# Two transformer blocks on one core: where the modulation's sums, the first attention steps and thirty adds of squares stand

## What is computed

```python
for l in range(2):                                     # first_block
    mod_x = silu(c) @ w_ada[l] + b_ada[l]              # 6 * 1024 columns
    mod_c = silu(c_ctx) @ w_ada[l] + b_ada[l]
    q, k, v... = modulate(rms_norm(x, g_norm1[l]), sh1, sc1) @ w_in[l]
    x = x + gt1 * (attention heads of three kinds @ w_out[l])
    x = x + gt2 * conv_ffn(modulate(rms_norm(x, g_norm2[l]), sh2, sc2), w_up, conv_w, w_down)
for l in range(2):                                     # second_block, 272 tokens
    h = h + 0.5 * rmsnorm(swiglu(rmsnorm(h, g_pre_ffn1[l]), ...), g_post_ffn1[l])
    h = h + rmsnorm(token_mixer(rmsnorm(h, g_pre_mix[l]), ...), g_post_mix[l])
    h = h + 0.5 * rmsnorm(swiglu(rmsnorm(h, g_pre_ffn2[l]), ...), g_post_ffn2[l])
```

## Time and profile before

| | |
|---|---|
| time, median of 3 runs | 2470.73 us (2468.18 to 2471.03) |
| the profiled execution | 2474.26 us, its span 2472.5 |
| mean granted TensorE clock | 0.975 |
| PE busy | 2346.7 us (95%) |
| DVE, ACT, POOL busy | 62%, 53%, 17% |
| wl splits (L1796) | 574, mean 1349 ns |
| POOL products (L744) | 50 of products_a, mean 2809 ns; 46 of products_b, mean 2642 ns |

### The profile page before, as it was taken

How to read it: one execution, slowest core, us unless ns; L and a number is a source line. 1 busy time by engine, 2 the same in 40 slices (tenths; PEclk the granted TensorE clock), 3 DMA queues, 4 the chain that set the end, 5 groups by cost and what they waited for, 6 DMA issues and landing times.

```text
span 2472.5 us, 46933 instructions
## 1 busy us (share of the span) xinstructions
PE 2346.7 (95%) x17349; PEld 2129.3 (86%) x17349; DVE 1530.2 (62%) x2405; ACT 1316.3 (53%) x2439; POOL 408.2 (17%) x348
## 2 busy tenths in 40 slices
PE   7999989999887999999999999999999999998998
PEld 5786768888665878999999888999999998898998
DVE  5436586666555555885665774676556647666764
ACT  4536556665555464655444646454454445555553
POOL 1214465652882031000000000000000000000000
PEclk9999989999998999999999999999999998999999
DMA  7750133434443302556555432445545563344654
GB/s 298 225 171 10 35 127 133 145 139 121 143 152 116 95 26 81 176 173 183 168 173 170 146 107 99 154 162 178 174 134 188 168 183 107 103 156 143 194 178 130
DMA packets 101200, 356.43 MB, mean 144 GB/s; under 512 B 11344, under 2 KB 13040, under 8 KB 101072
## 3 DMA queue, kind: packets, MB, share of 16 engines
q1 hardware_dynamic: 86704, 304.45, 38.2%
q0 software_dynamic: 14368, 50.24, 6.2%
HBM read 352.55 MB, written 1.05 MB: 143 GB/s over the span
## 4 chain that ended last, share of the span: by engine, by line
PE 76%; DVE 9%; POOL 5%; issue 4%; ACT 4%; DMA 1%; DVEq 1%; ACTq 0%; SPq 0%; POOLq 0%
PE ps L783 19%; PE ps L785 19%; PE ps L784 19%; POOL products_b L744 4%; DVE wl L1796 3%; PE ps L800 2%; PE ps L801 2%; PE ps L804 2%; PE ps L923 2%; PE ps L938 2%; PE ps L909 2%; ACT wh L1321 1%; DMA ada_raw<-in_w_ada 1%; PE ps L845 1%; DVE conv L2387 1%
## 5 line engine op out<-in xcount | busy, mean ns | idle before, releaser
L1796 DVE TENSOR_TENSOR wl<-raw,wh 128x1024 fp32r<-128x1024 f32 x574 | 773.5, 1349 | 560.7 <-ACT wh L1321 559.6
L783 PE MATMUL ps<-hH,wh 128*128 128x272 f32 (+2 forms) x2864 | 886.3, 309 | 9.5 <-DVE silu L2435 3.1
L784 PE MATMUL ps<-hL,wh 128*128 128x272 f32 (+2 forms) x2864 | 872.1, 305 | 0.0
L785 PE MATMUL ps<-hH,wl 128*128 128x272 f32 (+2 forms) x2864 | 871.9, 304 | 0.0
L1321 ACT ACTIVATE wh<-raw 128x1024 fp32r<-128x1024 f32 x574 | 602.3, 1052 | 256.9 <-PE ps L785 231.8
L783 PEld LDWEIGHTS ps<-hH,wh 128*128 128x128 f32 x2864 | 543.2, 190 | 41.6 <-issue 8.3
L784 PEld LDWEIGHTS ps<-hL,wh 128*128 128x128 f32 x2864 | 543.3, 190 | 19.9 <-issue 0.5
L785 PEld LDWEIGHTS ps<-hH,wl 128*128 128x128 f32 x2864 | 543.4, 190 | 19.0
L783 PE MATMUL ps<-actH,wh 128*128 128x272 f32 (+2 forms) x1136 | 347.9, 306 | 20.0 <-DVE wl L1796 19.0
L785 PE MATMUL ps<-actH,wl 128*128 128x272 f32 (+2 forms) x1136 | 347.3, 306 | 0.0
L784 PE MATMUL ps<-actL,wh 128*128 128x272 f32 (+2 forms) x1136 | 346.2, 305 | 0.0
(11 more groups left out here) (308 smaller groups left out, 3224.0 us busy)
## 6 DMA issues: line engine op xcount, KB each, us to landing
raw<-in_w_ffn_gu SPq DMA_DIRECT2D x176, 512.0 KB, 3.5
raw<-in_w_mix SPq DMA_DIRECT2D x98, 512.0 KB, 3.5
raw<-in_w_up SPq DMA_DIRECT2D x88, 512.0 KB, 3.5
raw<-in_w_ffn_down SPq DMA_DIRECT2D x64, 512.0 KB, 3.5
ada_rest<-in_w_ada POOLq DMA_DIRECT2D x32, 512.0 KB, 4.6
raw<-in_w_out SPq DMA_DIRECT2D x32, 512.0 KB, 3.4
raw<-in_w_down SPq DMA_DIRECT2D x32, 512.0 KB, 3.5
raw<-in_w_qk SPq DMA_DIRECT2D x26, 512.0 KB, 4.3
```

The lines of the kernel that those rows point to most:

```text
L783: pe.matmul(out, a_h, b_h, start=start, stop=False)
L784: pe.matmul(out, a_h, b_l, start=False, stop=False)
L785: return pe.matmul(out, a_l, b_h, start=False, stop=stop)
L1796: dve.tensor_tensor(wl[:, slot, :], raw[:, slot, :], wh[:, slot, :].bitcast(F32), ALU.subtract).then_inc(l_split, 1)
```

## The change

Three things. The modulation's sums are placed anew: three in out0 (steps 2, 4, 6), 28 in up0 (four in the first turn, three in each of the eight turns behind it) and 17 in down0 (two in three steps, and step 2); `SUM_EARLY` goes from 25 to 31. In attention, layer 0 has two early steps as layer 1 has, the second one's scores go to banks 2 and 3, and the attention's start waits for four tiles of v instead of five. And the six adds of squares of the five later pre-norms move from DVE to POOL (`add_squares`), each waiting for the add before it and for its square; POOL's memsets of the mixer's tables stand behind them.

```diff
--- before.py
+++ after.py
@@ -48,8 +48,9 @@
 ADA_FIRST = 2 * KT
 EARLY = 3
 RAW_AT = 8
-SUM_OUT, SUM_UP = 7, 18
-SUM_EARLY = SUM_OUT + SUM_UP
+SUM_OUT, SUM_UP = 3, 18
+SUM_EARLY = SUM_OUT + 3 * SUM_UP // 2 + 1
+SUM_DOWN = [j for j in range(24) if j % 3 < 2 or j == 2]
 DOWN_PARTS = (8, 8, 6)
 TILES2 = ((0, 16), (16, 128), (144, 128))
 GLA_LEVELS = 7
...
+        square_pooled = sem("square_pooled")
@@ -526,8 +528,8 @@
                 p = PAIRS[idx]
                 self.p, self.idx, self.qt, self.diff, self.m = p, idx, qt, p >= 6, m
                 self.n, self.g, self.bank = n, PAIR_STEPS[0] * l + n, 6 + idx % 2
-                self.early = n <= l
-                self.scores = 4 + 2 * n if self.early else 2 * (n % 2)
+                self.early = n <= 1
+                self.scores = 4 if n == 0 else 6 if l and n == 1 else 2 * (n % 2)
                 self.nk, self.k0 = (T1, 0) if qt < 2 else (TC, TX)
                 self.opens, self.closes = m == 0, p < 6 or m == 1
                 self.first, self.last = qt == 0 and m == 0, ends
@@ -756,6 +758,22 @@
                             pool.dma_start(weights[:, i % 2, :] if i < SUM_EARLY else weights_b[:, i % 2, :],
                                            io["w_ada"][1, i]).then_inc(weights_loaded[i % 2], 16)
 
+            squares_before = [0]
+
+            def add_squares(n):
+
+                for k in range(1, KT - 1):
+                    pool.wait_ge(sq_ready, 8 * n.idx + k + 1)
+                    if k > 1:
+                        pool.wait_ge(square_pooled, squares_before[0])
+                    ins = pool.tensor_tensor(n.nrstd[:, 0, n.lo:], n.nsq[:, 0, n.lo:] if k == 1 else n.nrstd[:, 0, n.lo:],
+                                             n.nsq[:, k, n.lo:], ALU.add)
+                    if k == KT - 2:
+                        ins.then_inc(sum_ready, 1)
+                    else:
+                        squares_before[0] += 1
+                        ins.then_inc(square_pooled, 1)
+
             pool.wait_ge(h_ready, 24)
             pool.dma_start(xT[:, :, X2:X0], io["metaT"].rearrange("(k p) t -> p k t", p=P)).then_inc(meta_loaded, 16)
             for l in range(2):
@@ -764,7 +782,7 @@
                 for dst, name in ((mask[:, T2 - P:T2], "causal"), (lmask[:], "lmask"), (wal[32:48], "wal%d" % l)):
                     src = io["w_alpha"][l].rearrange("r (t c) -> r t c", c=P) if name.startswith("wal") else io[name]
                     pool.dma_start(dst, src).then_inc(mix_tables, 16)
-                pool.wait_ge(x_tile, 8 * post_before[norms["post_ffn1", l].idx] + 8)
+                add_squares(norms["pre_mix", l])
                 pool.memset(xlev[:, 0], 1.0).then_inc(pool_set, 1)
                 pool.memset(xlev[:, 1], 1.0).then_inc(pool_set, 1)
                 pool.memset(cum_hl[:].bitcast(F32), 0.0).then_inc(pool_set, 1)
@@ -772,6 +790,9 @@
                 pool.memset(att[:], 0.0).then_inc(pool_set, 1)
                 pool.memset(att0[0:NMETA], 0.0).then_inc(pool_set, 1)
                 pool.memset(mask[:, 0:T2 - P], 0.0).then_inc(pool_set, 1)
+                add_squares(norms["pre_ffn2", l])
+                if l == 0:
+                    add_squares(norms["pre_ffn1", 1])
 
 
 
@@ -901,8 +922,10 @@
             def pair_attention(l):
                 def scores(st):
 
-                    if st.n >= 4 or st.n + l == 3:
+                    if st.n >= 4 - (l == 0):
                         pe.wait_ge(pair_exp, st.g - 1)
+                    if st.n == 2 + l:
+                        pe.wait_ge(*after_tile(S[f"v{l}"], 4))
                     b = st.scores
                     for qi, ki in ((0, 0), (0, 1), (1, 0)):
                         for c in range(2):
@@ -949,6 +972,8 @@
                         pe.wait_ge(qk_low, N_HEADT * l + 6)
                         pe.wait_ge(roped, N_ROPE * (l + 1))
                         pe.wait_ge(head_ln, N_HEADT * (l + 1))
+                    for t in range(3 * i * (1 - l)):
+                        pe.wait_ge(*after_tile(S[f"v{l}"], t))
                     scores(run[i])
 
                 yield early
@@ -1047,7 +1072,7 @@
                             rotated(N_HEADT - 1)
                     if i == 1 and t == 3:
                         early(0)
-                    if l == 1 and i == 2 and t == 0:
+                    if i == 2 and t == 1 - l:
                         early(1)
 
                 if l == 1:
@@ -1074,7 +1099,7 @@
                     pe.wait_ge(ada_row_ready, ADA_GROUPS)
                     turn_rows(7, ADA_GROUPS - 1, ada_rows)
 
-                for t in range(5):
+                for t in range(4):
                     pe.wait_ge(*after_tile(S[f"v{l}"], t))
                 pe.wait_ge(qk_low, N_HEADT * (l + 1))
                 pe.wait_ge(swap_ready, 64 * (l + 1))
@@ -1622,9 +1647,8 @@
                         head_root(N_HEADT - 1)
                     if i < 2:
                         head_high(N_HEADT - 2 + i)
-                    if i == 1:
-                        for st in pair_steps(l)[:l + 1]:
-                            exps(st)
+                    if i >= 1:
+                        exps(pair_steps(l)[i - 1])
 
                 act.preload_act_table_set("natural_log_exp_and_others")
                 for i in range(N_HEADT):
@@ -1670,8 +1694,8 @@
                         for v in range(2):
                             act.wait_ge(c_turned, v + 1)
                             act.activation(c_wide[:, v, :], ps[:, 4 + 2 * v, :], ACT.Copy).then_inc(c_wide_ready, 1)
-                    if l == 0 and s.j:
-                        sum_products(s.j - 1, products_a)
+                    if l == 0 and s.j in (2, 4, 6):
+                        sum_products(s.j // 2 - 1, products_a)
                 act.wait_ge(*after_tile(S[f"out{l}"], KT - 1))
                 square(n, KT - 1)
                 root(n)
@@ -1701,8 +1725,8 @@
                             round_act(s.k // 2 + 1, pair - 1)
                         act.wait_ge(conv_done, p0 + pair + 1)
                         act.activation(conv[:, r, 1, 0:tq], conv[:, r, 1, 0:tq], ACT.Silu).then_inc(silu_ready, 1)
-                        if l == 0 and not (isinstance(pair, int) and pair >= SUM_UP):
-                            sum_products(pair + SUM_OUT, products_a)
+                    if l == 0 and not (isinstance(s.j, int) and s.j >= 2 * SUM_UP) and (s.k or isinstance(s.i, int)):
+                        sum_products(s.i * 3 + (s.k + SUM_OUT), products_a)
                 round_act(FT - 1, FT - 1)
                 st = S[f"down{l}"]
                 act.preload_act_table_set("natural_log_exp_and_others")
@@ -1717,8 +1741,8 @@
                             gained(norms["pre_ffn1", 0], t)
                         else:
                             square(norms["n1", 1], t)
-                    if l == 0 and s.j < NADA - SUM_EARLY:
-                        sum_products(SUM_EARLY + s.j, products_b)
+                    if l == 0 and s.j in SUM_DOWN:
+                        sum_products(SUM_EARLY + SUM_DOWN.index(s.j), products_b)
 
 
             split(S["up1_0"], Step(0, 0, RING))
@@ -1849,8 +1873,6 @@
                 if n:
                     rest(n, KT - 1)
                     split(st, Step(0, 0, RING))
-                    for _ in range(KT - 2):
-                        add_square(n)
                     split(st, Step(0, 1, RING))
                     dve.wait_ge(root_ready, n.idx + 1)
 
@@ -2336,7 +2358,7 @@
                 rest_rows(13)
                 split(st, Step(0, 2, RING))
                 head_low(N_HEADT - 1)
-                for first in pair_steps(l)[:l + 1]:
+                for first in pair_steps(l)[:2]:
                     largest(first)
                 split(st, Step(0, 3, RING))
                 rest_rows(15)
```

## The result

The changed kernel takes 2483.36 us (median of 5 runs, 2478.13 to 2483.74) against 2470.93 for the kernel before, measured beside it: ratio 1.0047, 95% interval 1.0035 to 1.0059, so 12.4 us slower. The forecast was 2486.

What follows compares the result with a forecast made beforehand. PE was taken as the bound (busy 95%), its helpers having 0.4 us to spare per pair in the up projection. Terms −8 −26 +45 −3.5 +8 = +15.5 on the median 2470.73 gave 2486, range 2453 to 2499.

Steps and rivals of the forecast that it cites:

- Up projection: First layer's up projection, sums from 18 to 28: turns outgrow PE's 21.76 us; +45 in all, or +26.
- the walk: One up-projection turn followed instruction by instruction: third sum 16.1 us behind the first, turn 26.6 us (or 24.3).
- the worse end: Up projection: wl(3) waits for both halves of POOL's product, giving +45 rather than +26.
- 632.08: Profile row of the kernel before: a wl queued 1.45 us after a product began waited for both halves, taking 4.38.
- Rival 1: Up projection: wl slips between POOL's halves if queued over 2.0 us behind the product's start; −13.5, 2457; chance 0.27.
- Down projection: First layer's down projection, 23 sums before, 17 after: less idle and some clock; −26, or −31.
- the part put down to the clock: Norm's matmul behind the down projection: up to 2 us more gained with a shorter hole before it.
- Out projection: First layer's out projection, seven sums before, three after: −7 from PE's shorter wait, 1 for the clock; −8.
- Attention: First attention steps: layer 0's wait of 2.78 us goes, −3; layer 1 −0.5; together −3.5.
- Transitions: Five transitions, thirty adds moved to POOL: each excludes DVE for 0.63 us; +8, between 0 and 11.
- one of the signs: Transitions: PE would be seen waiting at chunk 3, with nh, xT and hL longer beside POOL's adds.
- Rival 2: Up projection: sums hide in ACT's 3.64 us idle and PE stays full; 2430 with free transitions; chance 0.09.

Runs made afterwards that it cites:

- products_memset: The changed kernel with each half product of POOL replaced by three memsets of the same buffer, leaving out the second layer's modulation; 2428.19 us.
- squares_only: The kernel before with only the adds of squares of the five later pre-norms moved to POOL; 2476.72 us, ratio 1.0018 to 1.0041.
- squares_memset: `squares_only` with each of its thirty POOL adds replaced by a memset of the same tile behind the same waits; 2469.89 us, ratio 0.9992 to 1.0016.
- idle_first_waits: The changed kernel with the middle sum in ACT's idle time, adds of squares on DVE, each turn's first product waiting for its first chunk's split; 2443.29 us.

## Why the prediction was right

**Up projection (+45 forecast, +43.2).** Right in mechanism and size: the first turn +7.1 (+7 forecast), the eight behind it +36.0 (+38), of which the first and the last were shorter than the walk. The turn of 26.6 was worked out from durations of before alone, and each instant of the walk is in the profile within 0.1 us. `products_memset` shows that POOL's reading is the cause: without it the turn is 22.3. The reason that I gave for choosing the worse end was incomplete, though, and that it led to the right end was luck: a distance of 1.44 us from the product's start to the queued split doesn't decide. At that distance there are splits that lose and splits that don't, and the length of POOL's half product before it separates most of them. The forecast hit since the row I picked, 632.08, happened to stand behind a delayed half, as the split in the walk does. Rival 1's point of decision, "over 2.0 us behind the product's start", isn't refuted: all 255 splits of the count that were queued so late went between. But it isn't needed either, since 75 went between from less.

**Down projection (−26, −23.6).** The wait at the fold shrank only from 9.70 to 6.41, and the norm behind it was no faster: the part put down to the clock, 2 us, didn't come. The granted clock is 0.50 at that norm in both kernels.

**Out projection (−8, −8.9)** as written: no add beside a product at the end, and the norm at the higher clock (1.12 for two matmuls at a granted clock of 1.00, instead of 2.07 at 0.50).

**Attention (−3.5).** −2.6 alone, −5.6 between the two profiles. The first has an interval that reaches to no change. At equal clock it is −1.9 to −3.2; the forecast had no term for the clock in the attention, and the rest of the −5.6 is mostly that.

**Transitions (+8, +6.8; +7.3 by `squares_only`).** Right in cause, and in size within the bounds, but not by the path that I gave. POOL's add took 0.74 to 0.98, not 0.63; it held DVE up by 0.5 to 0.6, 3.2 us in a transition (3.8 forecast). In none of the five does PE wait for chunk 3's split, which was one of the signs. It waits for hL in its first group, 0.2 to 0.3 us at a time, so what that split had to spare was the wrong thing to subtract. From norm to norm the five are longer by 2.4, 1.3, 0.3, 1.4 and 1.4, where the working had 3.4, 2.1, 1.1, 2.2 and 2.4 as the most. That it is the shared reading and not the order or the waits is shown by `squares_memset`. Here the rule of the Trainium skill, "SBUF — State Buffer", section "Who interferes with whom", held: two SBUF inputs on VectorE against a reading GpSimd instruction cost 0.5 us each time, against one that only writes nothing. Its rule that whoever issues first gets the pair is not what the 163 lost splits show: each was queued before the second half started.

**Rival 2** (the sums hide in the up projection) had almost no room: three products are 14.3 us of POOL reading, DVE's four splits and two pairs of actL and act another 7.6, together 21.9 in a turn of 21.76, if the two never read at once. The best order that was found, `idle_first_waits`, comes within 1.1 us of that. Whether one exists that keeps PE full wasn't shown either way.

## What to carry to other kernels

Count the time of two engines that exclude each other as if they were one: an instruction moved to an idle GpSimd is not free when VectorE is busy with two-input SBUF work beside it, and a sum placed where ScalarE is idle can still cost by the product it triggers. When the places of such work are chosen, look at which VectorE instruction meets which GpSimd instruction, and make GpSimd wait for the one that the bound engine needs; then look again, because the loss moves on, as it did three times here: twice to the next split, once to a sum that waited for the product held back. Replacing the suspect by a memset of the same tile behind the same waits tells the cost of sharing from that of order in one run.

## What the runs showed that was not expected

- Whether a queued VectorE split goes between two halves of a GpSimd product depends on what went before: always lost in 139 cases where GpSimd had gone straight on after a half that a split had stretched to 3.3 us, 3 of 48 lost where that half had taken 2.3 to 2.5. It was never lost in 275 cases where GpSimd had waited 1.3 us or more, but most of these were queued later as well. A memset of 0.16 us between the halves doesn't change it. What keeps this memory between the two engines wasn't found.
- A GpSimd add of 128x272 takes 0.79 or 0.96 us, in turns; a VectorE instruction that meets it takes 0.5 to 0.6 more.
- The granted clock fell to 0.50 at the start of layer 0's attention for 3.4, 6.9, 10.3 or 13.7 us in thirteen of the fourteen profiles, and not at all in the changed kernel. The attention is up to 4.6 us longer by it.
